# Second block's attention: up-projection copied ahead of a split and in three banks, last turned feature ahead of one, output's first part by features

## The reference, cut to what matters

```
proj = rms_norm(x, attn_norm) @ w_in            # splits into latent, "diff" and "chunk" parts
q    = rms_norm(c_q, q_norm) @ w_uq             # 6 heads: 64 features without, 32 with rotation
kv   = rms_norm(c_kv, kv_norm) @ w_ukv          # 128 latents -> 384 key and 384 value features
o_mla  = rms_norm(softmax(q k / sqrt(96)) v)    # 6 heads, chunk-causal
o_diff = rms_norm((softmax_0 - lam * softmax_1) v) # 6 heads, two maps each
o_ch   = rms_norm(softmax(q k / 8 + bias) v)    # 4 heads
x = x + concat(o_mla, o_diff, o_ch) @ w_out     # 1024 x 1024
x = x + conv_ffn(rms_norm(x, ffn_norm))
```

## Time and profile before

| | us |
|---|---|
| median of 3 runs | 1707.29 (1706.27 to 1708.68) |
| the profiled execution's own time | 1701.35 |
| its span, first to last instruction | 1699.9 |
| TensorE busy | 1593.0 (94%) |
| VectorE busy | 1049.2 (62%) |
| ScalarE busy | 805.3 (47%) |
| GpSimd busy | 238.5 (14%) |
| mean granted TensorE clock | 0.977 |

### The profile page before, as it was taken

How to read it: one execution, slowest core, us unless ns; L and a number is a source line. 1 busy time by engine, 2 the same in 40 slices (tenths; PEclk the granted TensorE clock), 3 DMA queues, 4 the chain that set the end, 5 groups by cost and what they waited for, 6 DMA issues and landing times.

```text
span 1699.9 us, 26871 instructions
## 1 busy us (share of the span) xinstructions
PE 1593.0 (94%) x10834; PEld 1382.0 (81%) x10834; DVE 1049.2 (62%) x1939; ACT 805.3 (47%) x1514; POOL 238.5 (14%) x284
## 2 busy tenths in 40 slices
PE   5899979999999999979899997888999998899998
PEld 3788758877777888867799986777999887689996
DVE  3633755565354435778787767666677656667765
ACT  1322872433233323558455544555555555556553
POOL 1200430010010100002011101132111012321110
PEclk8999999999999999999999998899999998999999
DMA  9467022262564224020356453324455533245452
GB/s 383 151 255 276 11 71 114 77 254 117 217 253 173 99 99 149 11 91 25 149 178 218 175 189 103 130 95 141 158 190 181 189 133 119 75 155 193 174 209 76
DMA packets 39418, 257.27 MB, mean 151 GB/s; under 512 B 5504, under 2 KB 6784, under 8 KB 10496
## 3 DMA queue, kind: packets, MB, share of 16 engines
q1 hardware_dynamic: 36416, 249.61, 40.4%
q0 software_dynamic: 1296, 4.72, 0.8%
q10 hardware_dynamic: 1584, 1.23, 0.3%
HBM read 254.49 MB, written 1.05 MB: 150 GB/s over the span
## 4 chain that ended last, share of the span: by engine, by line
PE 81%; DVE 9%; ACT 6%; issue 2%; DMA 1%; POOL 1%; SPq 0%; DVEq 0%; ACTq 0%
PE ps L473 24%; PE ps L474 23%; PE ps L475 23%; PE ps L489 2%; PE ps L640 2%; PE ps L627 2%; DVE wl L1709 2%; PE ps L618 2%; ACT wh L1277 1%; ACT arena L1621 1%; PE ps L1043 1%; ACT arena L1348 1%; PE ps L515 1%; DMA raw<-in_ev_w_in 1%; PE ps L599 1%
## 5 line engine op out<-in xcount | busy, mean ns | idle before, releaser
L1709 DVE TENSOR_TENSOR wl<-raw,wh 128x1024 fp32r<-128x1024 f32 (+2 forms) x328 | 383.0, 1209 | 379.5 <-ACT wh L1277 378.9
L1277 ACT CAST wh<-raw 128x1024 fp32r<-128x1024 f32 (+1 forms) x338 | 332.6, 1033 | 517.1 <-PE ps L475 398.5
L473 PE MATMUL ps<-xh,wh 128*128 128x256 f32 (+1 forms) x1582 | 495.4, 313 | 8.3 <-ACT arena L1578 8.0
L474 PE MATMUL ps<-xl,wh 128*128 128x256 f32 (+1 forms) x1582 | 490.0, 310 | 0.0
L475 PE MATMUL ps<-xh,wl 128*128 128x256 f32 (+1 forms) x1582 | 489.9, 310 | 0.0
L473 PEld LDWEIGHTS ps<-xh,wh 128*128 128x128 f32 x1582 | 303.4, 192 | 33.2 <-issue 9.2
L473 PE MATMUL ps<-wh,xh 128*128 128x512 f32 (+2 forms) x844 | 306.6, 363 | 21.6 <-DVE xl L2275 6.8
L475 PEld LDWEIGHTS ps<-xh,wl 128*128 128x128 f32 x1582 | 303.4, 192 | 15.3
L474 PEld LDWEIGHTS ps<-xl,wh 128*128 128x128 f32 x1582 | 303.5, 192 | 15.0 <-issue 0.7
L474 PE MATMUL ps<-wl,xh 128*128 128x512 f32 (+2 forms) x844 | 301.9, 358 | 0.0
L475 PE MATMUL ps<-wh,xl 128*128 128x512 f32 (+2 forms) x844 | 301.7, 357 | 0.0
(11 more groups left out here) (210 smaller groups left out, 1805.0 us busy)
## 6 DMA issues: line engine op xcount, KB each, us to landing
raw<-in_ada SPq DMA_DIRECT2D x48, 1024.0 KB, 6.8
raw<-in_up SPq DMA_DIRECT2D x44, 1024.0 KB, 6.0
raw<-in_fin SPq DMA_DIRECT2D x44, 1024.0 KB, 4.8
raw<-in_down SPq DMA_DIRECT2D x22, 1024.0 KB, 4.9
raw<-in_fout SPq DMA_DIRECT2D x22, 1024.0 KB, 4.9
raw<-in_win SPq DMA_DIRECT2D x12, 1024.0 KB, 4.9
raw<-in_ev_w_in SPq DMA_DIRECT2D x9, 1024.0 KB, 6.7
raw<-in_wout SPq DMA_DIRECT2D x8, 1024.0 KB, 4.8
```

The source lines that it names most:

```text
L473: e.matmul(out, A[0], B[0], start=first, stop=False)
L474: e.matmul(out, A[0], B[1], start=False, stop=False)
L1277: e.copy(hi_of(j)[:, a:b], raw_of(j)[:, a:b]).then_inc(*S.hi.up((j, half)))
L1709: e.tensor_tensor(lo_of(j)[:, a:b], raw_of(j)[:, a:b], hi_of(j)[:, a:b].bitcast(F), ALU.subtract).then_inc(*S.lo.up((j, half)))
```

## The change

1. `up_keys`: the three key products go to banks 6, 7 and 4 and the two value products to 6 and 7. Before, all five took turns in 6 and 7.
2. In iteration 3, ScalarE and VectorE copy the key and value products ahead of the cast and the subtraction of the weight chunk of that iteration. Before, they copied behind them.
3. In iteration 10, the high and the low part of the last turned diff block (feature block 5) stand ahead of the cast and the subtraction of the weight chunk. Before, they stood behind.
4. The output's diff part goes by feature blocks: iteration 11 makes block 4 for both halves of the tokens (tokens 128 to 255 first, in banks 0 and 1), iteration 12 block 5 for both and then block 3 for both. VectorE adds both halves to X in iteration 13, tokens 128 to 255 first. The mla part of feature block 2 begins with tokens 128 to 255 too.

```
--- before.py
+++ after.py
@@ -1001,16 +1001,14 @@
                 hv, lv = hi_of(j), lo_of(j)
                 wait_chunk(j)
                 wait_feature(("m", l), 2)
-                for g in range(3):
-                    b = bank()
+                for g, b in enumerate((6, 7, 4)):
                     wait_bank(b)
                     fs = slice(128 * g, 128 * g + 128)
                     m = mm3(ps[b][:, 0:256], (hv[:, fs], lv[:, fs]), (xh[:, 2, 256:512], xl[:, 2, 256:512]), True, True)
                     m.then_inc(*S.proj.up(("kn", l, g)))
                     BANK["kn", l, g] = b
                     free[b] = [(side[g % 2], ("kn", l, g))]
-                for t in t2:
-                    b = bank()
+                for t, b in enumerate((6, 7)):
                     wait_bank(b)
                     tk = slice(256 + 128 * t, 384 + 128 * t)
                     m = mm3(ps[b][:, 0:384], (xh[:, 2, tk], xl[:, 2, tk]), (hv[:, 384:768], lv[:, 384:768]), True, True)
@@ -1109,7 +1107,7 @@
 
             at = {"d": [(6, 7), (0, 1)], "m": [(6, 7), (0, 1)], "c": [(2, 3), (4, 5)]}
 
-            def out(name, t, ks, first, last, c):
+            def out(name, t, ks, first, last, c=None):
 
                 if first:
                     for b in at[name][t]:
@@ -1124,7 +1122,11 @@
                         wait_feature(("y", l), k)
                         m = mm3(ps[at[name][t][half]][:, :], (xh[:, k, tk], xl[:, k, tk]), (hv[:, ns], lv[:, ns]),
                                 first and k == ks[0], last and k == ks[-1])
-                    m.then_inc(*S.proj.up(("part", name, l, t, half), *([("use", J[f"wout{l}", c])] if half else [])))
+                    used = [("use", J[f"wout{l}", c])] if half and c is not None else []
+                    if last or name != "d":
+                        used.append(("part", name, l, t, half))
+                    if used:
+                        m.then_inc(*S.proj.up(*used))
                     if last:
                         free[at[name][t][half]] = [(S.vec, ("added", name, l, t, half))]
 
@@ -1162,9 +1164,15 @@
                     chunk_values(i - 8)
                 if i in TURN:
                     turned(TURN[i])
-                if i in (11, 12):
-                    out("d", i - 11, [3, 4, 5], True, True, 2)
-            for t in t2:
+                if i == 11:
+                    out("d", 1, [4], True, False)
+                    out("d", 0, [4], True, False)
+                elif i == 12:
+                    out("d", 1, [5], False, False)
+                    out("d", 0, [5], False, False, 2)
+                    out("d", 1, [3], False, True)
+                    out("d", 0, [3], False, True)
+            for t in (1, 0):
                 out("m", t, [2], True, False, 1)
             mean_square("m", range(3), 3)
             out("m", 0, [0, 1], False, True, 0)
@@ -1636,7 +1644,18 @@
                         q.wait_ge(*S.vec.at(("ms", "d", l, k - 2)))
                     e.activation(SQD[:, k % 2, :], ps[b][:, 0:256], ACT.Square).then_inc(*S.act.up(("sqd", l, k)))
 
+            def turned_high(i):
+                g = TURN[i]
+                q.wait_ge(*S.tr.at(("turned", l, g)))
+                high(("y", l), 3 + g, ps[BANK.get(("turned", l, g), 0)], vec("mix", 8 * l + 3 + g, 1))
+
             def beside(i):
+                if i == 3:
+                    copy2(("kn", l, 0), KN[:, 0, :])
+                    copy2(("kn", l, 2), KN[:, 2, :])
+                    copy2(("vm", l, 0), VM[:, 0, :])
+                elif i == 10:
+                    turned_high(i)
                 if i in (1, 2, 3, 4, 6, 8, 10):
                     weights(after({1: J[win, 5], 2: J[win, 6], 3: J[f"uq{l}", 0], 4: J[f"ukv{l}", 0], 6: J[win, 7],
                                    8: J[win, 8], 10: J[win, 9]}[i]))
@@ -1645,20 +1664,14 @@
                 elif i == 2:
                     for g in range(3):
                         copy2(("uq", l, g), QN[:, g, :], scale=qsc)
-                elif i == 3:
-                    copy2(("kn", l, 0), KN[:, 0, :])
-                    copy2(("kn", l, 2), KN[:, 2, :])
-                    copy2(("vm", l, 0), VM[:, 0, :])
                 elif i == 4:
                     copy2(((win, 7), 0), QC[:, 0, :], scale=-0.125)
                 elif i == 6:
                     copy2(((win, 8), 0), KC[:, 0, :])
                 elif i == 8:
                     copy2(((win, 9), 0), VC[:, 0, :])
-                if i in TURN:
-                    g = TURN[i]
-                    q.wait_ge(*S.tr.at(("turned", l, g)))
-                    high(("y", l), 3 + g, ps[BANK.get(("turned", l, g), 0)], vec("mix", 8 * l + 3 + g, 1))
+                if i in (6, 8):
+                    turned_high(i)
 
             for i in range(A.n + A.lag + 1):
                 if 0 <= i - A.lag < A.n:
@@ -2414,7 +2427,16 @@
                 q.wait_ge(*S.proj.at(("ms", name, l)))
                 e.tensor_scalar(r, ps[b][:, 0:2], 1.0 / n_, EPS, ALU.mult, ALU.add).then_inc(*S.vec.up(("ms", name, l)))
 
+            def turned_low(i):
+                g = TURN[i]
+                low2(("y", l), 3 + g, ps[BANK.get(("turned", l, g), 0)], vec("mix", 8 * l + 3 + g, 1))
+
             def beside(i):
+                if i == 3:
+                    copy2(("kn", l, 1), KN[:, 1, :])
+                    copy2(("vm", l, 1), VM[:, 1, :])
+                elif i == 10:
+                    turned_low(i)
                 if i in (1, 2, 3, 4, 10):
                     weights(after({1: J[win, 5], 2: J[win, 6], 3: J[f"uq{l}", 0], 4: J[f"ukv{l}", 0], 10: J[win, 9]}[i]))
                 if i == 1:
@@ -2425,20 +2447,17 @@
                         k = ("uq", l, 3 + g)
                         q.wait_ge(*S.proj.at(k))
                         e.tensor_tensor(QR[:, g, :], ps[BANK.get(k, 0)][:, 0:256], CSQ, ALU.mult).then_inc(*S.ev.up(k))
-                elif i == 3:
-                    copy2(("kn", l, 1), KN[:, 1, :])
-                    copy2(("vm", l, 1), VM[:, 1, :])
                 elif i == 5:
                     copy2(((win, 7), 1), QC[:, 1, :], scale=-0.125)
                 elif i == 7:
                     copy2(((win, 8), 1), KC[:, 1, :])
                 elif i == 9:
                     copy2(((win, 9), 1), VC[:, 1, :])
-                if i in TURN:
-                    g = TURN[i]
-                    low2(("y", l), 3 + g, ps[BANK.get(("turned", l, g), 0)], vec("mix", 8 * l + 3 + g, 1))
-                if i in (12, 13):
-                    add_part("d", i - 12)
+                if i in (6, 8):
+                    turned_low(i)
+                if i == 13:
+                    add_part("d", 1)
+                    add_part("d", 0)
 
             for i in range(A.n + A.lag + 1):
                 if 0 <= i - 1 < A.n:
```

## The result

The changed kernel takes 1695.39 us in the median of six runs (1693.53 to 1697.05), the kernel before 1708.93 (1706.27 to 1709.97). The ratio is 0.9923, with a 95% interval of 0.991 to 0.9936. 1697 was forecast. The two profiled executions differ by less, 1701.35 and 1695.38 us: the one of before that the prediction was worked out from was one of its quickest.

The account below looks back on a forecast made before the run. TensorE was taken to bound the second block's attention stages, its idle or half-rate time costing kernel time. Gains of 5.1 + 5.3 + 0 = 10.4 us from the 1707.29 us median gave 1697, range 1694.5 to 1699.5 (8 in 10: 1691.5 to 1702.5).

Parts of the forecast that it names:

- The three banks and the copies ahead of the split: Up-projection, layer 0: third key product starts at once, one 1.0 us pause; 4.3 us earlier, next iteration 3.1 more.
- What is late next: Behind the up-projection: later split delays VectorE's normalising; TensorE pauses 0.9 and 1.4 us before transposes of units 3 and 4.
- 5.1 and 5.3 us: Net gain by unit 4's transposes in layers 0 and 1, after the new pauses.
- 1.00 from 1086 to 1112: Sign of being right: TensorE's granted clock stays at full rate through that stretch of layer 0's attention stage.
- Rival (a): Clock still falls to 1.2 GHz for 10 us after the first short pause; total gain 5.4 us, 1702 us; chance 0.13.
- The end, counted at 0: Attention stage's end: waits sum to 4.46 us before and 4.5 after, same matmuls, so no gain; bounds 1 us either way.
- the 1.8 and 2.7 of the prediction: Waits at the stage's end: 1.8 us before unit 10's transposes, 2.7 us before the output's feature 2, for the addition.
- 10.4: Total forecast gain in us: 5.1 in layer 0, 5.3 in layer 1, 0 at the end.

Follow-up runs that it names:

- experiment 5: Kernel before with three banks alone for the key and value products, copies still behind the cast and subtraction: 1707.66 us, ratio 1.0004.
- experiment 6: Kernel before with the copies ahead of the cast and subtraction alone, products still taking turns in two banks: 1700.9 us, ratio 0.9957.
- experiment 2: Kernel before with the whole up-projection part alone, three banks and copies ahead of the split, end as before: 1697.12 us, ratio 0.9933.
- Experiment 7: Changed kernel with value halves copied behind the split, key blocks still ahead, next column in bank 6: 1689.4 us, ratio 0.9892 to the kernel before.
- experiment 8: Changed kernel with the diff part by token halves, feature blocks outermost (4, 5, 3), one addition per iteration: 1688.84 us, ratio 0.9884 to the kernel before.
- experiment 10: Kernel before with Experiment 7's up-projection, the end of the stage as before: 1695.06 us, ratio 0.9943.
- experiment 3: Kernel before with the end's part alone: turned block ahead of the split, diff part by feature blocks, additions together: 1705.65 us, ratio 0.9984.
- experiment 4: Kernel before with only the last turned block ahead of the split, diff part by token halves as before: 1708.13 us, ratio 0.9997.

## Why the prediction was right, point by point

**The three banks and the copies ahead of the split: right in mechanism.** The value products wait 0.92 us (1.0 forecast) for a copy that ScalarE makes behind its exponentials. From unit 3's scores to unit 2's transposes it takes 4.93 us, with 4.9 forecast. Experiments 5 and 6 share the credit out: banks alone nothing in the time, order alone all of the front but 0.35 us, and 6.3 of the 10.9 us that both gave in experiment 2.

**"What is late next" failed, in who is late first.** The prediction had the split 1.5 us later and looked behind it in VectorE's queue only: reciprocals, maxima, normalising, and so pauses of 0.9 and 1.4 us before the transposes of units 3 and 4. But the chunk being split is the weights of the very column that TensorE makes next. That column waited 1.44 us, and the transposes then waited for nobody. In the kernel before the chunk had been done at 1091.6 and its column began at 1097.80, so the trace showed no such wait; reading which chunk each cast in `beside` belongs to would have. Experiment 7 shows the wait to be this one. The pauses' sum was nearly right all the same: in experiment 8, where the clock stayed up, they are 1.43 and 0.51 us (at unit 4), and front is 5.1 and 5.3 us less than before, just as forecast. There VectorE's queue sets when unit 4 is ready, and the prediction had followed that queue; the pause that it missed only takes up waiting that it had put further on.

**"1.00 from 1086 to 1112" failed.** Behind that wait the clock is at half for 3.4 us per layer, which costs the 0.8 us between 17.88 and 17.07 us. Rival (a) had the mechanism, at another pause and for 10 us. So front is 4.3 us less where 5.1 was forecast, and 4.5 for 5.3. In weighing (a) the prediction took TensorE to be busy through all of the 10 us; the pause of 0.68 us before 1092.06 lies in them, and it is busy from there on.

**The end, counted at 0: right for the work, wrong for the clock.** The waits of 1.79 and 2.61 us are the 1.8 and 2.7 of the prediction, and where the clock stays up the old and the new end last the same: 64.86 and 64.83 us (before, experiment 7). In the changed kernel's trace a fall adds 1.5 us per layer. That the clock can fall at the old end's wait of 3.39 us too, as it did at 3.40 us in experiments 2, 5, 6 and 10, was not in the prediction at all.

**Why 13.5 us and not 10.4: open in part, and 1697 is luck in part.** The sum was made from one execution, 1701.35 us, and by it the changed kernel should take 1691 us; its profiled execution took 1695.38, because falls of the clock cost 0.8 us in each front and 1.5 us in each rest and left 5.9 of the 10.4 us. The same 10.4 us were then put on the median of before, and there they were too few, for 13.5 were measured. The two misses point opposite ways. In medians the parts add up: 10.9 us (experiment 2) and 2.3 us (experiment 3) are 13.2 of the 13.5.

What makes most executions of before longer than the two traced ones is not shown. One candidate is the clock at the end: every trace of the other kernels that make the diff part in the old order has falls there (experiments 2, 4, 5, 6 and 10: 1.3 to 2.8 us per layer above 64.85), and both traces of the unchanged kernel, of quick executions (1701 and 1703 us), have none. Three things speak against it as the whole cause. Experiment 10, with falls in both layers, spreads over 1.6 us only; experiment 8, without the long wait, over 5 us; and the traces here start unit 3's scores in layer 0, up to which all kernels are the same, anywhere between 1083.3 and 1086.9 us. The mean clock doesn't decide it: the kernel before took 1701.4 us in one execution and 1705.1 to 1705.8 in five others, all at 0.977, and those of 1709 us and more had 0.969 to 0.975. No slower execution of before was traced.

The Trainium skill, in "TensorE: Matmul & The Clock Gate", section "A second HAM failure mode: psum-queue depth-cycling", says that frequent short idle times between groups of matmuls, as banks are cycled, make the clock swing. The prediction gave that 0.13 against what the earlier trace rows showed; in the changed kernel's trace waits of 1.44 and 1.79 us did it, though these were for a weight chunk and for the normalising, not for a bank. It did not come each time: the 1.78 us wait of experiment 7 and the 1.43 us wait of experiment 8 lowered nothing.

## What to carry to other kernels

When copies are moved ahead of a weight split, follow the split's output to its first reader on TensorE, as well as the queue behind it: the cheapest order has ahead of the split only what TensorE waits for at once. When a wait is removed by reordering, add up the waits of the whole stage after it; work that is cut into shorter pieces ahead of a fixed point (unit 10's transposes here) only moves the wait, and experiment 8's order keeps the long piece there. And look at how the executions spread before putting a sum from one profile on their median.

## What the hardware showed

The length of a wait does not tell whether the granted clock falls. A wait of 3.39 us left it at 1.00 in both traces of the kernel before and took it to 0.50 in experiment 10 (3.40 us, both layers). One of 1.79 us took it down in the changed kernel and one of 1.78 us, behind the same instructions, did not in experiment 7. One of 1.44 us took it down in layer 0 of experiment 2 and one of 1.45 us did not in layer 1, and experiment 8 has the same wait in both layers without a fall. Once down, it stayed for 10.2 us in the kernel before, with TensorE busy all through from 1092.06 us on, and for 3.4 us in the changed one. What decides both is open. It isn't the instructions alone, since the two layers of experiment 2 have the same ones up to there.
